# A two-layer transformer block on one core: two query units as one token-stationary group, split fills, and three reorderings

## What is computed

```python
for l in range(DEPTH):
    u = _rmsnorm(h, ffn1_pre_g[l])
    h = h + 0.5 * _rmsnorm(_swiglu(u, w_gate, w_up, w_down), ffn1_post_g[l])
    u = _rmsnorm(h, mix_pre_g[l])
    y = _token_mixing(u, ...)              # four mixers, then y @ mix_w_out
    h = h + _rmsnorm(y, mix_post_g[l])
    u = _rmsnorm(h, xa_pre_g[l])
    m = _rmsnorm(mem, xa_mem_g[l])
    h = h + _rmsnorm(_cross_attention(u, m, w_q, w_kv, w_o), xa_post_g[l])
    u = _rmsnorm(h, ffn2_pre_g[l])
    h = h + 0.5 * _rmsnorm(_swiglu(u, ...), ffn2_post_g[l])
```

## Time and profile before

| | |
|---|---|
| median of 3 runs | 1283.72 us (1281.01 to 1283.88) |
| the profiled execution | 1280.59 us, of which the span is 1278.7 us |
| mean granted TensorE clock | 0.998 |
| TensorE busy | 98% of the span |
| VectorE, ScalarE, GpSimd busy | 64%, 52%, 17% |
| on the chain that ended last | PE 94%, DVE 3%, ACT 1%, issue 1% |
| transfers | 222.36 MB, 174 GB/s |

### The profile page before, as it was taken

One profiled execution on the slowest core, in us unless ns is written; L12 is line 12 of the kernel. 1 busy time (PEld: TensorE's weight loads), 2 busy tenths in 40 slices (PEclk: granted clock), 3 DMA queues, 4 the chain that ended last, 5 costly groups with the idle time before them and its releaser, 6 DMA issues.

```text
span 1278.7 us, 18589 instructions
## 1 busy us (share of the span) xinstructions
PE 1257.3 (98%) x6836; PEld 1069.4 (84%) x6836; DVE 815.4 (64%) x1169; ACT 660.9 (52%) x1099; POOL 212.9 (17%) x247
## 2 busy tenths in 40 slices
PE   8999999999999999999999999999999999999998
PEld 6888888899988888888888888788998798888886
DVE  5657767785656575555676566777857566755554
ACT  6454446664445464444564544565746455544442
POOL 1715441000002010000055243400000110100000
PEclk9999999999999999999999999999999999999999
DMA  9755444424525355555455555444255243655551
GB/s 349 263 197 176 175 174 149 165 100 171 192 83 198 105 228 197 197 188 179 167 193 181 193 197 197 163 151 163 68 196 188 79 182 132 233 182 181 178 185 62
DMA packets 32442, 222.36 MB, mean 174 GB/s; under 512 B 3584, under 2 KB 4096, under 8 KB 6784
## 3 DMA queue, kind: packets, MB, share of 16 engines
q1 hardware_dynamic: 30080, 209.28, 45.8%
q10 hardware_dynamic: 2304, 12.29, 2.5%
HBM read 219.46 MB, written 2.10 MB: 173 GB/s over the span
## 4 chain that ended last, share of the span: by engine, by line
PE 94%; DVE 3%; ACT 1%; issue 1%; DMA 0%; POOL 0%; SPq 0%; POOLq 0%; ACTq 0%; DVEq 0%
PE PS L1679 89%; PE PS L1796 2%; DVE w_lo L1151 1%; PE PS L2018 1%; PE PS L1822 1%; DVE mix_out L1151 0%; DMA raw<-in_weights 0%; DVE x_lo L1154 0%; ACT work L973 0%; ACT w_hi L681 0%; PE PS L2271 0%; PE PS L2062 0%; PE PS L2002 0%; PE PS L1949 0%; ACT x_hi L729 0%
## 5 line engine op out<-in xcount | busy, mean ns | idle before, releaser
L1151 DVE TENSOR_TENSOR w_lo<-raw,w_hi 128x1024 fp32r<-128x1024 f32 (+1 forms) x378 | 477.1, 1305 | 222.9 <-ACT w_hi L681 220.0
L681 ACT ACTIVATE w_hi<-raw 128x1024 fp32r<-128x1024 f32 x368 | 369.0, 1054 | 231.3 <-PE PS L1679 227.2
L1679 PE MATMUL PS<-w_hi,x_hi 128*128 128x512 f32 (+2 forms) x1104 | 426.0, 386 | 5.0 <-DVE x_lo L1154 2.6
L1679 PE MATMUL PS<-w_lo,x_hi 128*128 128x512 f32 (+2 forms) x1104 | 414.1, 375 | 0.0
L1679 PE MATMUL PS<-w_hi,x_lo 128*128 128x512 f32 (+2 forms) x1104 | 408.5, 376 | 0.0
L1679 PEld LDWEIGHTS PS<-w_hi,x_hi 128*128 128x128 f32 x1104 | 208.7, 189 | 46.5 <-issue 5.8
L1679 PEld LDWEIGHTS PS<-w_hi,x_lo 128*128 128x128 f32 x1104 | 208.6, 189 | 38.5
L1679 PEld LDWEIGHTS PS<-w_lo,x_hi 128*128 128x128 f32 x1104 | 209.1, 189 | 34.9 <-issue 0.5
L1679 PE MATMUL PS<-w_hi,hid_hi 128*128 128x512 f32 x336 | 131.5, 391 | 0.0
L1679 PE MATMUL PS<-w_lo,hid_hi 128*128 128x512 f32 x336 | 130.8, 389 | 0.0
L742 ACT ACTIVATE work<-PS,st 128x256 f32<-128x256 f32 x88 | 42.0, 478 | 155.0 <-PE PS L1679 153.5
(11 more groups left out here) (276 smaller groups left out, 1297.4 us busy)
## 6 DMA issues: line engine op xcount, KB each, us to landing
raw<-in_weights SPq DMA_DIRECT2D x194, 1024.0 KB, 4.7
pmat<-in_mats ACTq DMA_DIRECT2D x3, 1568.0 KB, 7.7
gain<-in_post ACTq DMA_DIRECT2D x8, 512.0 KB, 3.7
zone<-mem_scratch ACTq DMA_DIRECT2D x2, 1024.0 KB, 6.1
raw<-in_weights SPq DMA_DIRECT2D x3, 512.0 KB, 7.0
h<-in_x SPq DMA_DIRECT2D x2, 512.0 KB, 6.0
zone<-in_mem SPq DMA_DIRECT2D x1, 1024.0 KB, 9.9
mem_scratch<-zone ACTq DMA_DIRECT2D x1, 1024.0 KB, 5.8
```

What stands on the lines that cost most here:

```text
L681: a.activation(w_hi[s][:, c_], raw[s][:, c_], ACT.Copy).then_inc(sem[hi_done[s]], 1)
L1151: return v.tensor_tensor(o, x_, y_, op)
L1679: return t_.matmul(o, a_, b_, start=first, stop=last)
```

## The change

In words, per layer:

- POOL: the wait for `hid_t` 9 before `s_w[0]` (three operations of 128 x 1024) is gone, and `s_w[1]` waits for `hid_t` 9 in place of 10.
- DVE: `split_mid(22)` moves behind `attention_out(1)` and the phi activation. DVE and ACT: `split_mid(23)` moves ahead of the compressed attention's addition and squares. DVE: `split_mid(25)` moves ahead of the post-norm, and the splits of 28 and 29 come earlier against the softmax steps.
- The head of cross-attention is done by token tile, with sixteen fills of 128 columns on each of ACT and DVE; each fill list of the second tile ends behind the split of unit 26.
- Query units 0 and 1 become one 512-column group with the tokens stationary (`query_rows`: 2 token tiles x 8 row blocks x 3 matmuls of 512 columns), packed by rows as the gate and up units are. ACT copies both token tiles to `xq_tok`, TensorE transposes them with eight transposes (`xq_transposed`), ACT copies them to `proj`. Query units 2 and 3 are cut into halves j = 0, 1; the eight transposes stand between the halves of unit 2, the scores of head 0 before the first half of unit 3, those of head 1 between its halves.

```diff
+        xq_tok = v3(mix_out[:, 0:TT * 2 * UC], "p (t n) -> p t n", t=TT)
...
-        FILL = [0, 16, 32, 40, 48, 56, 60]
+        FILL = [0, 16, 32, 40, 48, 64, 68]
...
-        XT_AT = {0: 0, 1: 16, 2: 32, 3: 40}
-        ROW_BANK = (4, 5, 6, 7, 0, 1, 2, 3)
+        XT_AT = {0: 0, 1: 16, 2: 32, 3: 48}
...
                 tt(s_b[1], tb2, tb3, ALU.add)
                 brw, biw = bc(s_b[0], 2, CH), bc(s_b[1], 2, CH)
-                pool.wait_ge(*E.at("hid_t", 9))
-                pool.sem_inc(pool_held)
                 tw = v3(proj[:, 1280:2304], "p (g j c) -> p g j c", g=PAIRS, j=CH)
                 tt(s_w[0], brw, over_c(arj, CH, 0), ALU.mult)
                 tt(tw, biw, over_c(aij, CH, 0), ALU.mult)
                 tt(s_w[0], s_w[0], tw, ALU.subtract)
-                pool.wait_ge(*E.at("hid_t", 10))
+                pool.wait_ge(*E.at("hid_t", 9))
                 pool.sem_inc(pool_held)
                 tt(s_w[1], brw, over_c(aij, CH, 0), ALU.mult)
...
+                split_mid(23)
                 group_squares((1,), "cmp_done", 1)
-                split_mid(23)
                 act.wait_ge(*E.at("grp_t", 3))
                 mixer_hi(MO_ORDER[6:8])
                 split_mid(24)
                 split_mid(25)
                 y_squares(1)
+                fill_hi_of(2, 0, range(6))
                 h_square(2, 0)
-                fill_hi(2)
+                fill_hi_of(2, 0, (6, 7))
+                fill_hi_of(2, 1, range(6))
+                split_mid(M_Q + 2)
+                fill_hi_of(2, 1, (6, 7))
                 h_square(2, 1)
                 load_gain(2)
...
-                for q in range(4):
-                    m = M_Q + q
-                    split_mid(m + 2)
-                    s, n, _ = mid(l, m)
+                def xq_rows(t):
+                    if t == 0:
+                        act.wait_ge(*E.at("proj_half", 5))
+                    else:
+                        s, n, _ = mid(l, M_Q + 1)
+                        act.wait_ge(*E.at(unit_done[s], n + 1))
+                    a.activation(xq_tok[:, t], bank(4 + t), ACT.Copy).then_inc(sem["proj_done"], 1)
+
+                def xq_feature(q):
+                    s, n, _ = mid(l, M_Q + q)
                     act.wait_ge(*E.at(unit_done[s], n + 1))
                     a.activation(proj[:, q * 512:(q + 1) * 512], bank(4 + q % 2), ACT.Copy).then_inc(sem["xq_done"], 1)
-                    if q:
-                        xa_exp(q - 1)
+
+                xq_rows(0)
+                split_mid(M_Q + 3)
+                xq_rows(1)
+                split_mid(M_Q + 4)
+                act.wait_ge(*E.at("grp_t", 4))
+                for q in range(2):
+                    a.activation(proj[:, q * 512:(q + 1) * 512], bank(2 + q), ACT.Copy).then_inc(sem["xq_done"], 1)
+                xq_feature(2)
+                xa_exp(0)
+                split_mid(M_Q + 5)
+                xa_exp(1)
+                xq_feature(3)
+                xa_exp(2)
...
-                split_mid(22)
                 attention_out(1)
                 dve.wait_ge(*E.at("phi_t", 1))
...
                 stt(hx, hx2, 1.0, hx, ALU.add, ALU.mult).then_inc(sem["phi_hid"], 1)
+                split_mid(22)
                 split_mid(21)
                 attention_max(2)
                 mixer_lo(1)
...
                 attention_out(2)
+                split_mid(23)
                 dve.wait_ge(*E.at("cmp_o", 1))
                 tt(mo[:, :, 1], mo[:, :, 1], v3(bank(5), "p (t h d) -> p t h d", t=TT, h=H), ALU.add).then_inc(sem["cmp_done"], 1)
                 dve.wait_ge(*E.at("cmp_done", 1))
                 dve.wait_ge(*E.at("grp_sq", 2))
                 variance([(grp(ss, 1, 2), 256)])
                 group_norm(1, 1, 2)
-                split_mid(23)
                 mixer_lo(3)
                 split_mid(24)
-                post_norm(1, 1.0)
-                fill_lo(2)
                 split_mid(25)
+                post_norm_and_fill(1, 1.0, E.at, 2)
+                fill_lo_of(E.at, 2, 1, range(6))
+                split_mid(M_Q + 2)
+                fill_lo_of(E.at, 2, 1, (6, 7))
...
-                split_mid(M_Q + 2)
                 split_mid(M_Q + 3)
+                split_mid(M_Q + 4)
                 xa_max(0)
                 xa_probs(0)
-                split_mid(M_Q + 4)
+                split_mid(M_Q + 5)
                 xa_max(1)
                 xa_copy(0)
                 xa_probs(1)
-                split_mid(M_Q + 5)
                 xa_max(2)
                 xa_probs(2)
                 xa_copy(1)
...
-                rows_transposed(2)
+
+                def query_rows(t, half, at, between):
+                    s, _, ns = mid(l, M_Q + half)
+                    pe.wait_ge(*E.at(split_done[s], ns + 1))
+                    for k in range(KT // 2):
+                        if between and k == at:
+                            between()
+                        q = half * KT // 2 + k
+                        pe.wait_ge(*E.at("x_split", FILL[FI_XA] + KT * t + q + 1))
+                        c_ = slice(k * 2 * UC, (k + 1) * 2 * UC)
+                        i = three([(x_tile(q, t), (w_hi[s][:, c_], w_lo[s][:, c_]))], bank(4 + t), q == 0, q == KT - 1)
+                    return i
+
+                def second_rows():
+                    pe.wait_ge(*E.at("x_split", FILL[FI_XA] + KT))
+                    rows_of(2, 1, range(6))
+
+                def second_rows_end():
+                    pe.wait_ge(*E.at("x_split", FILL[FI_XA] + KT + 2))
+                    rows_of(2, 1, (6, 7))
+
+                keep_clock(7, 2)
+                rows_of(2, 0, range(6))
+                query_rows(0, 0, 0, None)
+                rows_of(2, 0, (6, 7))
+                query_rows(0, 1, 2, second_rows).then_inc(sem["proj_half"], 1)
+                s, _, _ = mid(l, M_Q)
+                query_rows(1, 0, 2, second_rows_end).then_inc(sem[unit_done[s]], 1)
+                s, _, _ = mid(l, M_Q + 1)
+                query_rows(1, 1, 0, None).then_inc(sem[unit_done[s]], 1)
...
-                def xa_query(q):
-                    s, n, ns = mid(l, M_Q + q)
-                    unit_feature(s, n, ns, bank(4 + q % 2), FI_XA if q == 0 else None)
+                def xa_query(q, j):
+                    s, _, ns = mid(l, M_Q + q)
+                    pe.wait_ge(*E.at("proj_done", 8 + q))
+                    pe.wait_ge(*E.at(split_done[s], ns + 1))
+                    for k in range(KT):
+                        c_ = slice(k * UC + j * P, k * UC + (j + 1) * P)
+                        i = three([((w_hi[s][:, c_], w_lo[s][:, c_]), (xh3[:, k], xl3[:, k]))],
+                                  bank(4 + q % 2)[:, j * S:(j + 1) * S], k == 0, k == KT - 1)
+                    if j == 1:
+                        i.then_inc(sem[unit_done[s]], 1)
+
+                def xq_transposed():
+                    pe.wait_ge(s_con, 16)
+                    pe.wait_ge(*E.at("proj_done", 11))
+                    for q in range(2):
+                        for k in range(2):
+                            for t in range(TT):
+                                i = t_.transpose(bank(2 + q)[:, k * S + t * P:k * S + (t + 1) * P],
+                                                 xq_tok[:, t, (2 * q + k) * P:(2 * q + k + 1) * P], ident)
+                    i.then_inc(sem["grp_t"], 1)
 
                 def xa_project(q):
                     s, n, ns = mid(l, M_O + q)
                     pe.wait_ge(*E.at("x_split", FILL[FI_XO] + q + 1))
                     unit_rows(s, ns, [(xh3[:, 2 * q + k], xl3[:, 2 * q + k]) for k in range(2)], q == 0, q == 3)
 
-                xa_query(0)
-                xa_query(1)
+                xa_query(2, 0)
+                xq_transposed()
+                xa_query(2, 1)
                 xa_scores(0)
-                pe.wait_ge(*E.at("xq_done", 1))
-                xa_query(2)
+                xa_query(3, 0)
                 xa_scores(1)
                 xa_transposed(0)
-                pe.wait_ge(*E.at("xq_done", 2))
-                xa_query(3)
+                xa_query(3, 1)
...
-        for q in range(4):
+        u = g["xa_w_q"][l][:, :2 * UC].reshape(KT, P, 2 * UC).transpose(1, 0, 2)
+        put(u[:, :KT // 2].reshape(P, UNIT))
+        put(u[:, KT // 2:].reshape(P, UNIT))
+        for q in (2, 3):
```

45 lines of the change are left out of this document (4 added, 41 removed).

## The result

| | before | after |
|---|---|---|
| median, runs taken side by side | 1282.37 us (1280.89 to 1283.88, 4 runs) | 1273.16 us (1273.08 to 1273.56, 4 runs) |
| the same two again, in another hour | 1280.63 us (1278.62 to 1286.42, 17 runs) | 1273.22 us (1272.42 to 1274.83, 6 runs) |
| span of the profiled execution | 1278.7 us | 1271.6 us |
| granted clock, mean | 0.998 | 1.000 |

The ratio is 0.9934, with a 95% interval of 0.9915 to 0.9952; taken again it is 0.9940 (0.9926 to 0.9954). The forecast was 1278.7 us (a ratio of 0.9961) with a range down to 1275.0.

The account below looks back on a forecast made before the run. It took the kernel as bound by TensorE, busy 1257.3 of 1278.7 us. Terms of 2.5 us a layer, 5.0 in all, take the profiled 1280.59 to 1275.6 us, or 1278.7 against the median 1283.72; range 1275.0 to 1282.1.

Parts of the forecast that it names:

- the sum: All terms added: 1.45 - 0.1 + 0.57 + 0.3 + 0.3 = 2.5 us a layer, 5.0 us in all.
- POOL's chain: End of first feed-forward: GpSimd done earlier, TensorE's 1.45 us wait goes; 0.1 us paid at the split near 157.
- The first rival: VectorE's clash stays at the split at 157.19: 2.4 of the 5.0 us lost, 1281.1 us; chance 0.10.
- Split 22: Mixer: moved behind attention_out(1), it removes TensorE's wait before the scores of attention 2; gain 0.57 us, bounds 0.4 and 0.57.
- Split 23: Mixer: moved into VectorE's 3.41 us gap, it shortens TensorE's 0.59 us wait for x_lo; gain 0.3 us, bounds 0 and 0.59.
- The head of cross-attention: Fillers to query unit 2: 16.15 us with the added transposes in place of 16.48; gain 0.3 us a layer.
- The second rival: Cross-attention's head: first query matmul as late as now, each layer loses 1.4 us, 1282.1 us; chance 0.11.
- the third: Cross-attention's head goes as well as in the feed-forward: gain 1.1 in place of 0.3 us, 1277.1 us; chance 0.12.
- the fourth: ScalarE's copies for head 0's scores wait on a late load: up to 4.7 us a layer, 1288.1 us; chance 0.03.

Follow-up runs that it names:

- the orders: Kernel before with the POOL edit and the moves of splits 22 and 23, cross-attention as before: 1273.65 us, the second time 1274.26 us.
- The filler in the wait of 0.57 us: Kernel before with one filler (two matmuls of 256 columns) on TensorE ahead of its wait before the scores of attention 2: 1280.65 us, ratio 0.9996.
- the filler ahead of the 16: Kernel before with one filler ahead of the 16 matmuls of 15 columns: 1279.87 us; with three there and three behind the one-column matmuls: 1283.83 us.
- split 24: Changed kernel with split 24 moved ahead of the last pieces of the mixer's output, on VectorE and ScalarE: 1271.68 us, ratio 0.9926.
- the kernel with the hole: Changed kernel with split 22 back ahead of attention_out(1) and its first half made twice: 1285.81 us, ratio 1.0037.

## Why the prediction was right in kind and wrong in size

Against the median of three runs, 1283.72 us, the gain is 10.5 us, and 5.0 were forecast. It divides so: 5.8 us are waits and work of TensorE, by the stages; 1.9 us are clock (2.3 us lost before, 0.4 after); and 2.9 us are the difference between that median and the one of 84 runs. Against the forecast, 1278.7 us, the kernel came 5.5 us early: 0.8 us by the stages, 1.9 us by the clock, and the rest by the level from which the sum started. The step that failed is **the sum**, in two places.

- It was made against the trace's idle time alone, and had no term for TensorE's clock. The profile said 0.998, and the view by windows of layer 1 would have shown the 3.4 us at 990.8. I read layer 0 and doubled it; the two layers differ by 1.59 us in one stage, and that difference was the part of the missing term that this profile held. Most of the lost clock went with the very edit that I put down at 0.57 us, split 22's move.
- "It lies 3.1 us under the median of the three runs, so against the median" was carried over as a constant. But that median of three lies 2.9 us over the one of 84, and the profiled execution 0.2 us under it. That two of the three had lost more to the clock is likely, by the 84; their own clocks are not on record. The changed kernel loses little there, so its time should have been summed from the full-clock level up.

Point by point:

- **POOL's chain**: 1.45 less 0.1 was 1.35; 1.61 to 1.63 us were measured. No TensorE wait came at 163, and the pair took 4.96 us where 5.4 was forecast, so the 0.1 was not paid. The other 0.16 is how the idle column counts: it starts at the end of the matmul before the wait, and without the wait the transposes start 0.17 us ahead of that end (191.28, where the matmuls at 190.83 end at 191.45). The first rival (6.97 us) did not come. The rule of the Trainium skill on the shared read interface (SBUF — State Buffer, Who interferes with whom) holds in kind: the clash moved with the products, to splits with slack. The forecast had only the one at 157 and missed the next, 2.2 us longer. And GpSimd paid as well: its first two operations took 2.7 us each in place of 1.92.
- **Split 22**: 0.57, measured 0.63, the same surplus over the idle column as at POOL's chain; and 0.15 more in the stage behind it, 0.10 of that the short wait behind the thin matmuls. The second wait has no term in the sum.
- **Split 23**: 0.3, measured 0.13 alone. TensorE's wait for `x_lo` is 0.44 us where I forecast 0.3; splits 22 and 23 together were 0.87 in the sum and are 0.63 and 0.26 in the stages, 0.89.
- **The head of cross-attention**: 3.0 us from fillers to the first query matmul, measured 2.98; 16.15 us with the transposes, measured 15.27 and 0.85, 16.12. The gain was to be 0.3 and is 0.35 on top of the orders. The second rival (loss of 1.4) and the third (gain of 1.1) did not come, nor did the fourth: no load was late.

Their sum, 2.5 us a layer, stands against 2.9; the mechanisms of the waits were right. From the kernel's time at full clock, 1278.5, less the 5.0 of the sum, the forecast would have been 1273.5.

What stays open is what split 22's move takes away that matters to the clock. The filler in the wait of 0.57 us fills that wait and does not save the clock. But it leaves the short wait behind the 16 thin matmuls (1.98 and 1.99 us to the wide one), which the move and the filler ahead of the 16 remove, and the stretches behind the 16 came only where it stood. That 0.1 us by itself makes the clock fall is not shown: the fillers ahead of the 16 also added wide work, and the stretches fall in some passes and not in others. A filler between the 16 and the wide matmul would test it. What POOL's chain alone gained beyond its stages stays open too.

## What to carry to other kernels

Cut the trace at the same landmarks in every layer before summing: two layers with the same work that differ by over 0.1 us hold a term that the waits don't show. Where the granted clock is under 1 and executions spread more than 0.3%, find the stretch at 1.2 GHz, and price a short wait beside thin matmuls with the clock that may hang on it; work out the time at full clock first, and forecast from there. A split that must be done somewhere belongs in its engine's idle time ahead of the critical piece, as split 24 here, and not behind that piece.

## What the runs showed of the hardware

- TensorE fell to 1.2 GHz while busy for the whole of a stretch (6.80 of 6.80 us at 291.3), behind matmuls of 65 and of one column with no wait among them. With six wide matmuls beside the thin ones, at two places in each layer, the mean clock was 0.999 or more in ten of 12 executions.
- Behind 16 matmuls of 15 columns it fell in 6 of 14 layers where the next matmul came 1.98 to 2.01 us after their start, and in none of 20 where it came 1.88 us after (the kernel with the hole left out). One stretch of 3.4 us costs 1.5 to 1.6 us.
- A hole of 1.83 us ahead of the scores (matmuls with 64 rows) was followed by 10.2 us at 1.2 GHz in one layer and 6.8 us in the other. A hole of 1.45 us ahead of 128-column transposes and 512-column matmuls had no such effect.
- The two waits cost TensorE a little more than their idle column: 0.63 for 0.57 us, 1.61 for 1.45 us, since a matmul that does not wait starts before the one ahead of it ends.
- VectorE and GpSimd slowed each other: two pieces of a split took 4.96 us in place of 2.35, and two GpSimd operations 2.69 and 2.68 in place of 1.92.
